# A transformer block on one core: shorter router chain, gate blocks of the first pass ahead of the shared up blocks, and an opening of the weight ring that uses three slots twice

## What is computed

```python
def route(xf, w_router, bias):
    s = jax.nn.sigmoid((xf @ w_router).astype(jnp.float32))
    sel = s + bias.astype(jnp.float32)
    grp = sel.reshape(t, N_EXPERT_GROUPS, N_EXPERTS // N_EXPERT_GROUPS)
    gscore = lax.top_k(grp, 2)[0].sum(-1)
    _, gidx = lax.top_k(gscore, TOPK_GROUPS)
    ...
    _, idx = lax.top_k(jnp.where(emask, sel, -jnp.inf), TOP_K)
    w = jnp.take_along_axis(s, idx, axis=-1)
    w = w / jnp.sum(w, axis=-1, keepdims=True) * ROUTED_SCALE
    return idx, w
...
    g = jnp.einsum("td,edf->tef", xf, p["w_exp_gate"])
    u = jnp.einsum("td,edf->tef", xf, p["w_exp_up"])
    a = jax.nn.silu(g) * u * comb[..., None].astype(xf.dtype)
    routed = jnp.einsum("tef,efd->td", a, p["w_exp_down"])
    shared = (jax.nn.silu(xf @ p["w_sh_gate"]) * (xf @ p["w_sh_up"])) @ p["w_sh_down"]
```

## Time and profile before

| | us |
|---|---|
| median of 3 runs | 1091.15 (1090.59 to 1092.48) |
| the profiled execution's own time | 1088.44 |
| its span, first to last instruction | 1086.5 |
| PE busy | 999.6 (92%) |
| DVE busy | 550.9 (51%) |
| ACT busy | 224.9 (21%) |
| mean granted TensorE clock | 0.986 of full |
| moved by DMA | 380.39 MB, mean 350 GB/s |

### The profile page before, as it was taken

One profiled execution on the slowest core, in us unless ns is written; L12 is line 12 of the kernel. 1 busy time (PEld: TensorE's weight loads), 2 busy tenths in 40 slices (PEclk: granted clock), 3 DMA queues, 4 the chain that ended last, 5 costly groups with the idle time before them and its releaser, 6 DMA issues.

```text
span 1086.5 us, 15430 instructions
## 1 busy us (share of the span) xinstructions
PE 999.6 (92%) x5980; PEld 558.6 (51%) x6003; DVE 550.9 (51%) x1088; ACT 224.9 (21%) x453; POOL 23.8 (2%) x33
## 2 busy tenths in 40 slices
PE   3999999999999999999999999979899898998985
PEld 2544588888875454444584554433343333433421
DVE  3100387775865774985571426534445445444434
ACT  5311120000002471000520303311212203213213
POOL 1000010000002001000000000000000000000002
PEclk9999999999999999999999999999999999999998
DMA  9999999999874747998659999999999999999995
GB/s 356 391 389 389 363 337 364 376 365 328 287 293 155 261 164 253 387 324 305 208 195 389 398 409 407 408 409 406 409 408 407 409 407 409 408 407 409 409 407 201
DMA packets 158653, 380.39 MB, mean 350 GB/s; under 512 B 10530, under 2 KB 44144, under 8 KB 157424
## 3 DMA queue, kind: packets, MB, share of 16 engines
q1 hardware_dynamic: 158576, 379.35, 92.7%
HBM read 377.22 MB, written 2.10 MB: 349 GB/s over the span
## 4 chain that ended last, share of the span: by engine, by line
PE 65%; DMA 13%; SPq 11%; DVE 5%; issue 3%; ACT 2%; ACTq 0%; POOL 0%; DVEq 0%; POOLq 0%
PE ps L674 64%; DMA ring<-in_w_exp_down 7%; SPq L544 5%; SPq L549 5%; DMA ring<-in_w_mod 3%; DVE part L1695 2%; DMA ring<-in_w_exp_up 2%; DMA qkv<-in_w_mod 1%; DVE xres L2177 1%; PE ps L997 0%; PE ps L761 0%; ACT nreg L1508 0%; DVE tiny L1889 0%; ACT ring L1501 0%; SPq L555 0%
## 5 line engine op out<-in xcount | busy, mean ns | idle before, releaser
L674 PE MATMUL ps<-nreg,ring 128*128 128x256 f32 (+2 forms) x1312 | 304.9, 397 | 2.5 <-issue 1.2
L674 PEld LDWEIGHTS ps<-nreg,ring 128*128 128x128 f32 (+1 forms) x1312 | 242.6, 189 | 62.2 <-issue 28.1
L1695 DVE SCALAR_TENSOR_TENSOR part<-ring,csT,part 128x512 f32<-128x512 f32 x232 | 174.7, 753 | 11.0 <-DVE part L1695 0.5
L674 PE MATMUL ps<-ring,nreg 128*32 128x512 f32 (+1 forms) x1344 | 173.9, 600 | 3.4 <-DMA ring<-in_w_exp_up 2.9
L674 PE MATMUL ps<-ring,conv 128*32 128x512 f32 (+2 forms) x688 | 101.8, 647 | 24.4 <-DMA ring<-in_w_exp_down 24.4
L674 PE MATMUL ps<-ring 128*128 128x512 f32 x256 | 110.7, 592 | 0.0
L674 PEld LDWEIGHTS ps<-ring,nreg 128*32 128x32 f32 (+1 forms) x1344 | 49.2, 114 | 110.9 <-issue 110.8
L2177 DVE TENSOR_TENSOR xres<-xres,ps 128x512 f32<-128x512 f32 x96 | 62.0, 684 | 44.6 <-PE ps L674 44.6
L674 PEld LDWEIGHTS ps<-ring 128*128 128x128 f32 x256 | 48.6, 190 | 60.4 <-issue 60.0
L674 PEld LDWEIGHTS ps<-ring,conv 128*32 128x32 f32 (+2 forms) x688 | 30.1, 123 | 87.6 <-issue 83.6
L674 PE MATMUL ps<-pick,qnT 128*128 128x128 bf16 x384 | 67.0, 220 | 2.4 <-DMA ring<-in_w_exp_up 2.4
(11 more groups left out here) (287 smaller groups left out, 851.1 us busy)
## 6 DMA issues: line engine op xcount, KB each, us to landing
ring<-in_w_mod SPq DMA_DIRECT2D x78, 1024.0 KB, 11.1
ring<-in_w_exp_gate SPq DMA_DIRECT2D x128, 512.0 KB, 13.4
ring<-in_w_exp_up SPq DMA_DIRECT2D x128, 512.0 KB, 15.1
ring<-in_w_exp_down SPq DMA_DIRECT2D x128, 512.0 KB, 14.5
ring<-in_w_in SPq DMA_DIRECT2D x12, 2048.0 KB, 12.7
ring<-in_w_out SPq DMA_DIRECT2D x8, 2048.0 KB, 10.4
ring<-in_w_mod SPq DMA_DIRECT2D x3, 2048.0 KB, 17.5
ring<-in_w_in SPq DMA_DIRECT2D x3, 1664.0 KB, 16.2
```

The costliest lines, as they stand in the source:

```text
L674: return nc.tensor.matmul(o, l, r, start=start, stop=stop)
L1695: ins = V.scalar_tensor_tensor(out=out_, in0=w_, scalar=scale, in1=acc_, op0=ALU.mult, op1=ALU.add)
```

## The change

1. **Router.** Two DVE instructions that zero the scores of the other groups go. The five doubling steps, the addition, the comparison and the product become two `tensor_tensor_scan` instructions of 32 elements and one fused instruction. Each partition's own expert size (`own`) now comes from 8 small matmuls (32 columns of weights, 32 moving) instead of a product and a sum on DVE; the slot numbers, the only thing that the first sort matmul needs, raise `sort_in` before the blocks are made.
2. **Shared gate.** `first_gates` runs the two first gate blocks side by side over k, and `sh_gate` rises three times for them: when both are half done, when block 0 is done, when block 1 is done. `shared_silu(n)` waits for n + 2.
3. **First pass.** PE runs 13 steps of `shared_up(1, 0)` around `gather(0, (0, 1))`, then block q = 0 at once. The other 3 steps, all of `shared_up(1, 1)` and banks 2 and 3 of the gather stand between the gate blocks. The up blocks write PSUM banks 6 and 7 instead of 2 and 3. `shared_act` moves behind `tokens_out` on DVE.
4. **Ring.** `PLACE` opens with indexes 0, 1, 2, 0, 1, 2 before index 3 is used; before it opened with 0, 1, 2, 3, 0, 1, 2, 3.

Its core (of `PLACE` the two lines, of the router the parts that are new):

```diff
-PLACE = [2 * s + h for s in (0, 1, 2, 3, 0, 1, 2, 3, 0, 1, 4, 2, 3, 0, 1, 4, 2, 3, 0, 5) for h in range(2)]
+PLACE = [2 * s + h for s in (0, 1, 2, 0, 1, 2, 0, 3, 1, 2, 4, 0, 3, 1, 2, 4, 0, 3, 1, 5) for h in range(2)]
...
-            def first_room(s):
+            def first_room(s, half):
                 if s == 1:
-                    sp.wait_ge(sh_gate, 2)
+                    sp.wait_ge(sh_gate, 1 if half == 0 else 3)
...
-                    sp.wait_ge(sh_gate, 4)
+                    sp.wait_ge(sh_gate, 5)
...
-                bank = ps[:, 2 * i + m, 0:T] if m < 2 else ps[:, 2 + m, T * i:T * i + T]
+                bank = ps[:, 6 * i + m, 0:T] if m < 2 else ps[:, 2 + m, T * i:T * i + T]
...
-                if ks[-1] == KC - 1:
+                if ks[-1] == KC - 1 or (i == 0 and m == 1 and ks[-1] == KC // 2 - 1):
...
-            shared_up(0, 0)
+            def first_gates(ks):
+
+                for k in ks:
+                    for m in range(2):
+                        shared_up(0, m, (k,))
+
+            first_gates(range(0, 5))
+            shared_up(0, 0, (5,))
             pe.wait_ge(mask_ready, 1)
+            for t in range(2):
+                mm(ps[:, 4, 0:32], ones, mask[:, t, :], t == 0, t == 1)
+            for t in range(2):
+                for q in range(4):
+                    ins = mm(ps[32 * q:32 * q + 32, 4, 32:64], mask[:, t, :], ones[:, 0:32], t == 0, t == 1)
+            ins.then_inc(rank_full, 1)
...
+            shared_up(0, 1, (5,))
+            shared_up(0, 0, (6,))
...
+            first_gates(range(8, KC))
+            pe.wait_ge(rank_ready, 1)
+            shared_up(1, 0, range(0, 11))
             pe.wait_ge(split_ready, 4)
             pe.wait_ge(sh_silu, 2)
             gather(0, (0, 1))
-            shared_up(1, 1, range(10, KC))
-            pe.wait_ge(sh_act, 1)
...
-                    if base == 0 and q == 3:
+                    if base == 0 and q == 1:
+                        shared_up(1, 0, range(13, KC))
+                        gather(0, (2,))
+                    elif base == 0 and q == 2:
+                        shared_up(1, 1, range(0, 8))
+                        gather(0, (3,))
+                    elif base == 0 and q == 3:
+                        shared_up(1, 1, range(8, KC))
                         shared_up(0, 2)
+                        pe.wait_ge(sh_act, 2)
...
-                sc.wait_ge(sh_gate, n + 1)
+                sc.wait_ge(sh_gate, n + 2)
...
-            gm = tiny[:, 104:112]
-            link(V.tensor_scalar(gm, tiny[:, 104:112], 1.5, None, ALU.is_lt))
...
+            link(V.tensor_reduce(greater, mask[:, :, :], AX.X, ALU.add))
+            for t in range(2):
+                ins = V.tensor_tensor_scan(seen[:, t, :], ones[:, 0:NE], ties[:, t, :], greater[:, t:t + 1], ALU.mult, ALU.add)
             link(ins)
-            V.tensor_copy(sel[:, :, :], scan[:, 0, :, :])
-            link(V.tensor_reduce(tiny[:, 120:122], mask[:, :, :], AX.X, ALU.add))
-            for n, d in enumerate((1, 2, 4, 8, 16)):
-                a, b = scan[:, n % 2, :, :], scan[:, (n + 1) % 2, :, :]
-                V.tensor_copy(b[:, :, 0:d], a[:, :, 0:d])
-                link(V.tensor_tensor(b[:, :, d:NE], a[:, :, d:NE], a[:, :, 0:NE - d], ALU.add))
-            link(V.tensor_tensor(scan[:, 1, :, :], scan[:, 1, :, :], tiny[:, 120:122].unsqueeze(2).to_broadcast([P, 2, NE]),
-                                 ALU.add))
-            link(V.tensor_scalar(scan[:, 1, :, :], scan[:, 1, :, :], TOP_K + 0.5, None, ALU.is_lt))
-            link(V.tensor_tensor(sel[:, :, :], sel[:, :, :], scan[:, 1, :, :], ALU.mult))
+            link(V.scalar_tensor_tensor(out=sel[:, :, :], in0=seen, scalar=TOP_K + 0.5, in1=ties, op0=ALU.is_lt, op1=ALU.mult))
...
+            copied = mark(V.tensor_copy(rtmp[:, 6 * NE:7 * NE + 1], ps[:, 4, 0:NE + 1]))
...
+            placed = mark(V.scalar_tensor_tensor(out=slots0, in0=ps[:, 5, 0:64].rearrange("p (t e) -> p t e", t=2),
+                                                 scalar=1.0, in1=mask[:, :, :], op0=ALU.add, op1=ALU.mult))
+            ve.wait_ge(v_step, compared)
+            ranked = mark(V.tensor_reduce(tiny[:, 121:122], both, AX.X, ALU.add))
+            ve.wait_ge(v_step, placed)
+            V.tensor_scalar(slots0, slots0, -1.0, None, ALU.add).then_inc(sort_in, 1)
...
+            tokens_out(0, 1)
             shared_act(0)
-            tokens_out(0, 1)
+            tokens_out(0, 3)
             shared_act(1)
-            tokens_out(0, 3)
```

More of the change, by code:

```diff
@@ L572, in room @@
                 if not TURN[n]:
-                    first_room(RING[PLACE[n] // 2])
+                    first_room(RING[PLACE[n] // 2], PLACE[n] % 2)
                 else:
@@ L1124, in _ @@
             gather(0, (0, 1))
-            shared_up(1, 1, range(10, KC))
-            pe.wait_ge(sh_act, 1)
+            shared_up(1, 0, range(11, 13))
             def wait_units(ns):
@@ L1196, in gate_up @@
                         wait_over(job)
-                    if base == 0 and q:
-                        if q == 1:
-                            pe.wait_ge(sh_act, 2)
-                        if q < 3:
-                            gather(0, (q + 1,))
                     if q == 1 and kind != "over":
@@ L2026, in _, with mark @@
-            link(V.tensor_tensor(scan[:, 1, :, :], scan[:, 1, :, :], tiny[:, 120:122].unsqueeze(2).to_broadcast([P, 2, NE]),
-                                 ALU.add))
-            link(V.tensor_scalar(scan[:, 1, :, :], scan[:, 1, :, :], TOP_K + 0.5, None, ALU.is_lt))
-            link(V.tensor_tensor(sel[:, :, :], sel[:, :, :], scan[:, 1, :, :], ALU.mult))
+            def mark(ins):
+                steps[0] += 1
+                ins.then_inc(v_step, 1)
+                return steps[0]
+            last_ = [top8[:, 8 + t, TOP_K - 1:TOP_K] for t in range(2)]
@@ new lines, in _ @@
+            ties, seen, greater = scan[:, 0, :, :], scan[:, 1, :, :], tiny[:, 120:122]
+            for t in range(2):
+                ins = V.tensor_scalar(mask[:, t, :], sel[:, t, :], last_[t], None, ALU.is_gt)
+            masked = mark(ins)
+            for t in range(2):
+                V.tensor_scalar(ties[:, t, :], sel[:, t, :], last_[t], None, ALU.is_equal)
+            ve.wait_ge(v_step, masked)
+            link(V.tensor_reduce(greater, mask[:, :, :], AX.X, ALU.add))
+            for t in range(2):
+                ins = V.tensor_tensor_scan(seen[:, t, :], ones[:, 0:NE], ties[:, t, :], greater[:, t:t + 1], ALU.mult, ALU.add)
@@ L2030, in _ @@
+            link(ins)
+            link(V.scalar_tensor_tensor(out=sel[:, :, :], in0=seen, scalar=TOP_K + 0.5, in1=ties, op0=ALU.is_lt, op1=ALU.mult))
             V.tensor_tensor(mask[:, :, :], mask[:, :, :], sel[:, :, :], ALU.add).then_inc(mask_ready, 1)
             ve.wait_ge(mask_ready, 1)
+            cnt, own = rtmp[:, 6 * NE:7 * NE], rtmp[:, 7 * NE:7 * NE + 1]
+            fewer, equal, both = scan[:, 1, 0, :], scan[:, 1, 1, :], rtmp[:, 8 * NE:10 * NE]
+            slots0 = vrow[:, 0:64].rearrange("p (t e) -> p t e", t=2)
@@ L2037, in _ @@
-            link(ins)
-            ve.wait_ge(rank_full, 1)
-            cnt, own = scan[:, 0, 0, :], scan[:, 0, 1, :]
-            link(V.tensor_copy(cnt, ps[:, 5, 64:96]))
-            slots0 = vrow[:, 0:64].rearrange("p (t e) -> p t e", t=2)
-            V.scalar_tensor_tensor(out=slots0, in0=ps[:, 5, 0:64].rearrange("p (t e) -> p t e", t=2),
-                                   scalar=1.0, in1=mask[:, :, :], op0=ALU.add, op1=ALU.mult)
-            link(V.tensor_tensor(own, cnt, sum4, ALU.mult))
@@ L2046, in _ @@
-            V.tensor_scalar(slots0, slots0, -1.0, None, ALU.add)
-            link(V.tensor_reduce(tiny[:, 120:121], own, AX.X, ALU.add))
-            fewer, equal = scan[:, 1, 0, :], scan[:, 1, 1, :]
-            V.tensor_scalar(fewer, cnt, tiny[:, 120:121], None, ALU.is_gt)
-            link(V.scalar_tensor_tensor(out=equal, in0=cnt, scalar=tiny[:, 120:121], in1=tie, op0=ALU.is_equal, op1=ALU.mult))
-            link(V.tensor_tensor(fewer, fewer, equal, ALU.add))
-            link(V.tensor_reduce(tiny[:, 121:122], fewer, AX.X, ALU.add))
+                V.tensor_scalar(tbl[:, 2 + t, :], comb[:, t, :], tiny[:, 126 + t:127 + t], ROUTED_SCALE, ALU.mult, ALU.mult)
@@ L2058, in _ @@
             V.tensor_scalar(sums[:, 0:NE], blocks[:, 0:NE], expert_of, None, ALU.mult)
-            V.tensor_scalar(sums[:, NE:2 * NE], blocks[:, 0:NE], tiny[:, 120:121], None, ALU.mult).then_inc(sort_in, 1)
+            V.tensor_scalar(sums[:, NE:2 * NE], blocks[:, 0:NE], own, None, ALU.mult)
             ve.wait_ge(sort_full, 1)
```

30 lines of the change are left out of this document (13 added, 17 removed).

## The result

| | before | changed |
|---|---|---|
| median of the runs timed side by side, us | 1090.64 (8 runs, 1088.23 to 1095.19) | 1093.70 (8 runs, 1092.22 to 1096.27) |
| the profiled execution's own time | 1088.44 | 1094.55 |
| its span | 1086.5 | 1092.6 |
| mean granted TensorE clock | 0.986 | 0.977 |

The changed kernel is slower: ratio 1.0031, 95% interval 1.0017 to 1.0044, 3.1 us by the medians. The two profiled executions lie 6.1 us apart, since the one of before is among its quickest and the one of after above its median. So the traces tell where the time goes, and the medians tell how much it is. One run of the kernel before beside experiments 1 to 4 took 1326.32 us at a mean clock of 0.755 and is left out of their ratios.

The account below looks back on a forecast made before the run. DMA's expert-weight stream bounds the kernel, with PE only 0.4 us ahead at unit 38. PE loses 6.4 us, regains 2.8, less 0.4 ahead: +3.2; profiled 1088.44 becomes 1091.6, median forecast 1094.4 us, range 1089.8 to 1096.6.

Parts of the forecast that it names:

- The split waits for a silu: Before the gather: ACT's copies follow a silu due at 555.9, split ends at 564.6, PE idles 3.4 us.
- The router's chain is worth nothing by itself: DVE's router: table written about 4 us earlier, but the stream still waits for slot 3; 0.9 us left at the split.
- PE's lateness goes to the end: At unit 38, first in slot 0: PE 3.6 us later, less 0.4 ahead, moves stream and end by +3.2 us.
- The clock: After PE's wait before the gather: granted clock falls, costing 1.6 us, bounds 0 and 1.7.
- the wait comes, the clock holds: Rival at the split: PE waits but its clock does not fall; +1.6 us, 1092.8 us; chance 0.14.
- The small matmuls: 8 added router matmuls on PE, 16 records at 0.06 each: 0.96 us, bounds 0.2 and 2.1.
- The mask wait: PE after 11 shared gate steps waits 0.45 us for the router's mask, against 0.41 before.
- The wait for unit 8: PE's 2.38 us wait at 583.35 goes, because gate blocks start later than their units land.
- PE's work is otherwise the same, only in another order: PE from 539.19 to the end of the second pass's up blocks: no further cost beyond the listed terms.

Follow-up runs that it names:

- experiments 1 to 4: Changed kernel with copies before silu, 0.9993; kernel before with new router chain alone, 0.9999; changed kernel with split wait filled by unused matmuls, 1.0016; before with new PLACE alone, 1.0072.
- Experiment 1: Changed kernel with ACT's two copies to hb moved ahead of the first silu; median 1089.41 us, ratio 0.9993 to before.
- experiment 2: Kernel before with the new router chain and its PE matmuls alone, old blocks, ring and silu; median 1090.21 us, ratio 0.9999.
- experiment 5: Kernel before with 5 unused matmuls (4.3 us) ahead of the second pass's shared up block; median 1094.28 us, ratio 1.0033.
- experiment 6: Changed kernel with slot 0 entering the ring one place pair later (units 40 and 41 instead of 38 and 39); median 1092.93 us, ratio 1.0019.
- experiment 10: Changed kernel run again without an edit, with a second profile; median 1092.94 us, ratio 1.003 to before, profiled execution 1091.0 us.
- experiment 4: Kernel before with the new ring table PLACE alone; median 1097.99 us, ratio 1.0072.
- experiment 8: Kernel before with unused matmuls ahead of PE's two last waits in the last pass; median 1090.76 us, ratio 1.0002.
- experiment 7: Changed kernel with copies to hb ahead of the first silu and unused matmuls ahead of PE's two last waits; median 1088.42 us, ratio 0.9981 to before.

## Why the prediction was right, and where it was not

It said 1094.4 us and slower; it is 1093.7, and +3.1 where the sum had +3.2. The steps one by one:

- **The split waits for a silu.** As forecast. The silu ran at 555.51 (forecast 555.9), the split ended at 564.0 (564.6), PE stood still 3.42 us (3.4). Experiment 1 removes this one cause and the loss is gone.
- **The router's chain is worth nothing by itself.** So it came out in experiment 2, but not for the forecast's reason alone: the late sum of the final norm, 1.4 us in that trace, comes with the new router code and the prediction has no term for it. The mask came at 544.46 (544.5), and the scans took 0.23 each, as taken. The first issue went at 549.74 (550.2), unit 4 at 564.60 (565.2).
- **PE's lateness goes to the end.** Right in size, and experiment 5 shows the path by itself: unit 38 was issued at 659.06 (659). The place was wrong. The sum takes the stream as running until unit 38 and charges PE's lateness there, less 0.4. In the changed kernel the stream was 3.6 us late by 640, and unit 38 made no hole (399 GB/s from 655 to 662); experiment 6 issues it 7 us earlier and gains nothing that is clear of noise. The lateness passed into the stream at unit 6 and about units 18 to 22, which the prediction names as short of room and counts as part of the same term.
- **The clock.** 1.6 was taken; the profile after has 1.6 by the granted clock and 1.4 by the length of the gather. But it is no constant: behind the same wait experiment 10 has no fall, and experiment 6 loses 2.4 us in the gather alone (5.10 against 2.69), above the forecast's bound of 1.7. The forecast's rival "the wait comes, the clock holds" is not another outcome but a part of the executions' spread; it gave +1.6, and that execution of the changed kernel issues unit 38 1.6 us late. The traces here have seven waits of PE of over 2 us in the first two passes. The clock fell behind 5.47 (experiment 4), 3.42 (changed), 3.42 (experiment 6) and 2.33 (experiment 8), and did not behind 3.42 (experiment 10), 2.54 (experiment 5) and 2.38 (before). The Trainium skill, "TensorE: Matmul & The Clock Gate", section "Why this matters for your kernels", warns of gaps between bursts. Two of the three waits of 3.42 agree with it, and the one of experiment 10 does not. The same page of the Trainium skill, section "What's actually happening", says of the slow matmuls at a kernel's start that their number varies from run to run of the same kernel; the traces here show such a variation in the middle of a kernel too.
- **The small matmuls: too high.** 0.96 was taken from a row of 0.06 per record. The 16 records took 545.08 to 545.34, 0.26 us from first start to the next block's, 0.016 each. The mask's matmuls around them became longer too: the whole group, from its first start to the next step, takes 1.51 us instead of 1.14, so the 8 small ones cost 0.37. The estimate by the floor that the Trainium skill states, 0.4, was the better one.
- **The mask wait: too high**, 0.27 instead of 0.45.
- **The wait for unit 8: not gone whole.** The prediction had it vanish because the gate blocks start later than their units land. In the profile after, 0.70 is left at 585.17: the slow clock delayed the first gate block, unit 6 waits for that block, and so unit 8 came late as well. In experiment 10 it is gone. The step that failed is that the clock was charged once, on PE, though it delays a transfer too.
- **"PE's work is otherwise the same, only in another order": not quite.** The same 80 steps of the shared blocks took 35.64 us instead of 35.25, counted from start to start, 35.63 in experiment 10. They stand in more and shorter groups now; that this is the reason was not tested.

With the measured sizes the lateness is 0.27 + 3.42 + 1.44 + 0.37 + 0.70 + 0.39 = 6.6 less 2.8, so 3.8, where 3.6 was forecast: the errors were of both signs and cancelled. The traces have 3.85 at unit 38, of which 0.07 was there at PE's first shared step. For experiment 10 the same terms without the clock and the wait for unit 8 give 1.6, and its unit 38 is 1.6 late.

That +3.1 was measured where +3.2 was forecast is in part luck. The forecast has no term for the late sum of the final norm, 1.3 to 1.5 us. An estimate from the traces: the loss at the end is some 3.4 + 1.4 = 4.8 us where the clock falls after the split and 1.2 + 1.4 = 2.6 where it holds, if each carries what PE is late beyond 0.4; the median of the executions lies between.

The two profiled executions are 6.1 us apart: 3.85 at unit 38, 5.1 where PE gets past its last wait for an up weight (1052.63 before, 1057.75 changed), and the rest behind ACT's last record, where the late sum costs 1.4 and the end of the program gives back 0.4. Why 1.3 us are added between unit 38 and that last up weight is open; with one execution on each side it may be chance.

Open too is why the DMA engines show a busy share near 1.00 while they move less. From 576 to 620 all seven traces with the new order of blocks have 375 to 381 GB/s, and the kernel before and experiments 2 and 5 have 397 to 402 (392 in experiment 8, whose clock fell). The slow stretches lie about SP's waits for room: from 604 to 608 the changed kernel moves 311 and then 264 GB/s in 2 us each.

## What to carry to other kernels

When a semaphore's values get a new meaning, look up on each in-order queue not only who waits for the value but what stands behind the waiting instruction. Here the silu lost nothing by waiting 9 us, and the two copies behind it held DVE, PE and SP in turn. A head start is worth only what the next wait of the same queue leaves of it: follow it through every wait that ties the bound engine to another. A late issue is not yet a hole: look whether the transfers stopped there. And compare the end of the program in both traces too, even where nothing was edited; here 1.4 us stood there. Where an idle gap of PE can't be closed, filling it with matmuls nobody needs held the clock for those behind it: it gave about 2 us at the split, some 1 us at the end of experiment 7, and nothing at the end of the kernel before, where the filling took as long as it saved.
